# Moving the work between the matrix products of two mixer layers into and beside other stages

## The reference, cut to what matters

```python
h = rmsnorm(x, norm1_g[l])
u = einsum('btd,de->bte', h, w_in[l])                  # 3592 columns
(mq, mk, mv, mo, mi, mf, aq, ak, av, hq, hf, hi, hg) = split(u)
y_m = mlstm_mixer(mq, mk, mv, mo, mi, mf, ...)          # 4 heads of 64
y_a = diff_attention(aq, ak, av, ...)                   # 4 heads of 2 maps of 64, values of 128
y_h = hgrn2_mixer(hq, hf, hi, hg, ...)                  # 4 heads of 64
x = x + einsum('bte,ed->btd', concat([y_m, y_a, y_h]), w_out[l])
h2 = rmsnorm(x, norm2_g[l])
x = x + einsum('btf,fd->btd', square(relu(h2 @ w_up[l])), w_down[l])
```

## Time and profile before

| | us |
|---|---|
| median of 3 runs | 4036.71 (4032.25 to 4044.81) |
| the profiled execution | 4039.2 |
| its span, first to last instruction | 4037.4 |
| PE busy | 3690.6 (91%) |
| DVE, ACT, POOL busy | 1445.7, 1004.3, 1495.3 |
| DMA | 360.53 MB, mean 89 GB/s |

### The profile page before, as it was taken

How to read it: one execution, slowest core, us unless ns; L and a number is a source line. 1 busy time by engine, 2 the same in 40 slices (tenths; PEclk the granted TensorE clock), 3 DMA queues, 4 the chain that set the end, 5 groups by cost and what they waited for, 6 DMA issues and landing times.

```text
span 4037.4 us, 41511 instructions
## 1 busy us (share of the span) xinstructions
PE 3690.6 (91%) x16098; PEld 2831.0 (70%) x16098; DVE 1445.7 (36%) x2693; ACT 1004.3 (25%) x1287; POOL 1495.3 (37%) x557
## 2 busy tenths in 40 slices
PE   8999998899999998999998986679999986679999
PEld 7878785488878886457887873346888873346887
DVE  5453477242434223332101167442110167442110
ACT  2222324322222222022222233222222233222221
POOL 3445540144545453004455421013555420014553
PEclk9999998999999999899999997669999997669999
DMA  6434220143534331202222220002222220002221
GB/s 243 182 147 151 94 77 18 53 156 130 198 109 178 131 125 62 84 21 84 90 100 92 84 73 1 0 6 78 94 94 101 86 73 1 0 11 73 95 104 73
DMA packets 53861, 360.53 MB, mean 89 GB/s; under 512 B 5968, under 2 KB 6352, under 8 KB 16592
## 3 DMA queue, kind: packets, MB, share of 16 engines
q1 hardware_dynamic: 53712, 358.53, 24.5%
HBM read 356.41 MB, written 2.10 MB: 89 GB/s over the span
## 4 chain that ended last, share of the span: by engine, by line
PE 84%; DVE 10%; ACT 3%; issue 2%; POOL 1%; DMA 1%; SPq 0%; DVEq 0%; POOLq 0%; ACTq 0%
PE LP L424 74%; PE XB L424 8%; DVE rstd L1444 1%; DVE ada_in L1444 1%; PE XB L614 1%; DVE S L1636 1%; DMA big<-w_ada 1%; PE LP L730 1%; ACT L892 0%; ACT sq L892 0%; DVE big L1883 0%; ACT E L892 0%; DVE tmp L1767 0%; DVE st L1765 0%; POOL S L1324 0%
## 5 line engine op out<-in xcount | busy, mean ns | idle before, releaser
L1248 POOL TENSOR_TENSOR w_lo<-ring,w_hi 128x2048 fp32r<-128x2048 f32 (+1 forms) x263 | 1124.6, 4276 | 697.3 <-ACT w_hi L892 696.2
L424 PE MATMUL LP<-u_hi,w_hi 128*128 128x512 f32 x2480 | 989.0, 399 | 21.2 <-ACT u_hi L892 17.0
L424 PE MATMUL LP<-u_hi,w_lo 128*128 128x512 f32 x2480 | 979.1, 395 | 0.0
L424 PE MATMUL LP<-u_lo,w_hi 128*128 128x512 f32 x2480 | 936.8, 390 | 0.0
L424 PE MATMUL LP<-big_r,w_hi 128*128 128x512 f32 x2432 | 749.7, 389 | 1.2 <-POOL w_lo L1248 1.2
L892 ACT ACTIVATE w_hi<-ring 128x2048 fp32r<-128x2048 f32 (+1 forms) x263 | 468.9, 1783 | 965.2 <-PE LP L424 877.6
L424 PEld LDWEIGHTS LP<-u_hi,w_hi 128*128 128x128 f32 x2480 | 474.8, 191 | 124.6 <-issue 26.4
L424 PEld LDWEIGHTS LP<-u_hi,w_lo 128*128 128x128 f32 x2480 | 474.4, 191 | 101.6
L424 PEld LDWEIGHTS LP<-u_lo,w_hi 128*128 128x128 f32 x2480 | 466.5, 188 | 95.5 <-issue 0.5
L424 PEld LDWEIGHTS LP<-big_r,w_hi 128*128 128x128 f32 x2432 | 456.0, 188 | 95.6 <-issue 1.3
L424 PE MATMUL LP<-big_r,w_lo 128*128 128x512 f32 x1216 | 473.2, 389 | 0.0
(11 more groups left out here) (237 smaller groups left out, 3479.6 us busy)
## 6 DMA issues: line engine op xcount, KB each, us to landing
ada_in<-w_ada SPq DMA_DIRECT2D x66, 1024.0 KB, 4.9
ring<-w_in SPq DMA_DIRECT2D x22, 1024.0 KB, 4.8
ring<-w_gu00a SPq DMA_DIRECT2D x11, 1024.0 KB, 7.1
ring<-w_gu00b SPq DMA_DIRECT2D x11, 1024.0 KB, 6.7
ring<-w_gu01a SPq DMA_DIRECT2D x11, 1024.0 KB, 6.7
ring<-w_gu01b SPq DMA_DIRECT2D x11, 1024.0 KB, 6.6
ring<-w_gu10a SPq DMA_DIRECT2D x11, 1024.0 KB, 6.7
ring<-w_gu10b SPq DMA_DIRECT2D x11, 1024.0 KB, 6.9
```

The costliest lines, as they stand in the source:

```text
L424: return pe.matmul(o, lhsT=lhsT, rhs=rhs, start=start, stop=stop)
L1248: gp.tensor_tensor(w_lo[:, slab % RING, 0:width], ring[:, slab % RING, 0:width], w_hi[:, q % 2, 0:width].bitcast(F32), ALU.subtract).then_ ...
```

## The change

- `in` is loaded and computed in another order (`IN_ORDER`): gates first, then aq and ak, hf, hq, mq, mk, hg, mo. Its loop is unrolled.
- In the middle of a slab (`amid`) and behind it (`after`) PE gets small products. In `in`: slabs 2 to 5 rotate two chunks of q or k each and sum the squares of two; slabs 5 to 7 spread the eight inverse norms. The norms are kept as 8 rows (`half_sums` is a [128, 8] weight), so that Sqrt and RECIPROCAL work on [8, 512]; the norm's gain is applied where the slab is taken out, and the inverse norm is multiplied in behind the rotation.
- The gates, the recurrence's sigmoids, logarithm and sums, the convolutions and silus follow their slabs.
- The recurrence works on both pairs of heads at once (tiles of [128, 2, 512], `Z`). Levels 0 to 7 stand behind slabs 7 to 10 of `in` and 0 to 3 of `inv`, with the two halves j taken in turn (16 matmuls a level). Levels 8 and 9 and the product with v are placed in attention, behind the scores of units 0, 2, 4 and 6, in `LP[1]`.
- The mlstm loop uses `LP[0]`, `LP[1]`, XB[0] to XB[2]; `den` is a matmul with 4 columns of weights. The norms of attention's output and of the recurrence stand in this loop as 8 rows (`mix_norms`: 6 matmuls of sums behind unit 5, 6 of spreading behind units 8 to 13).
- `wo` no longer waits for everything: the 12 matmuls of slab 0 and then of slab 1 that don't use mlstm's chunks run while its division and norm are worked out as 4 rows.

What it takes away: `square_sums`, `root_one`, `rms_each`, `norm_qk`, the ten steps for each cp, the waits and norms between the stages.

The diff, cut to its core:

```diff
+                def qk_sums(pair):
+                    pe.wait_ge(s("qk_squared"), 4 * l + pair + 1)
+                    if pair == 2:
+                        pe.wait_ge(s("qk_root"), 2 * l + 1)
+                    for i in range(2):
+                        c = 2 * (pair % 2) + i
+                        last = mm(XB[0][0:8, :], half_sums(c, 8), big[:, 22 + c, :], start=c == 0, stop=c == 3)
+                    if pair % 2:
+                        last.then_inc(s("qk_summed"), 1)
+                def qk_spread(i):
+                    if i % 4 == 0:
+                        pe.wait_ge(s("qk_recip"), 2 * l + i // 4 + 1)
+                    if i == 0:
+                        pe.wait_ge(s("a_taken"), l + 1)
+                    else:
+                        pe.wait_ge(s("qk_scaled"), 8 * l + (i if i < 5 else i - 1))
+                    mm(XB[0 if i in (5, 7) else 3][:, :], halves_of(i % 4), qk_rows(i // 4)).then_inc(s("qk_spread"), 1)
...
+                def level(step):
+                    if step:
+                        pl.got("z_ready")
+                    else:
+                        pe.wait_ge(s("qk_scaled"), 8 * (l + 1))
+                        pl.got("h_k")
+                        pl.got("h_q")
+                    for cp in range(2):
+                        if step:
+                            pe.wait_ge(s("level_taken"), 2 * (8 * l + step - 1) + cp + 1)
+                        z = Z[:, 2 * (step % 2) + cp, :]
+                        for b in range(NB):
+                            for j in range(2):
+                                r, bank = half(j), XB[2 * cp + j]
+                                if step == 0:
+                                    last = mm(bank[:, blk(b)], big[r, SP + cp, blk(b)], big[r, HQ + cp, blk(b)])
+                                else:
+                                    last = mm(bank[:, blk(b)], z[r, blk(b)], z[r, blk(b)])
+                        last.then_inc(s("level_mm"), 1)
+                def amid_slab(k):
+                    if k == 5:
+                        qk_spread(1)
+                    if 2 <= k < 6:
+                        slab_taken(k - 1)
+                        rotate((AQ + 2 * k - 4, AQ + 2 * k - 3), cc("rot16"))
+                        qk_sums(k - 2)
...
+                        qk_spread(6)
+                        qk_spread(7)
+                def behind_slab(k):
+                    if k == 4:
+                        qk_spread(0)
+                    if k == 5:
+                        qk_spread(2)
+                    if k == 6:
+                        qk_spread(4)
+                        qk_spread(5)
+                    if k >= 7:
+                        level(k - 7)
+                linear(f"in{l}", "fm", src, after=behind_slab, fresh=fresh, amid=amid_slab)
+                linear(f"inv{l}", "tm", src, after=lambda k: level(k + 4))
...
+                def far_levels(n):
+                    if n == 0:
+                        pl.got("z_ready")
+                        for cp in range(2):
+                            for b in range(2):
+                                for j in range(2):
+                                    z = Z[half(j), cp, :]
+                                    o = 256 * cp + P * b
+                                    last = mm(LP[1][:, j, o:o + P], z[:, blk(2 * b)], z[:, blk(2 * b + 1)])
+                        last.then_inc(s("far_mm"), 1)
+                    if n in (2, 4):
+                        cp = n // 2 - 1
+                        if cp == 0:
+                            pl.got("z_ready")
+                        pe.wait_ge(s("far_taken"), 3 * l + cp + 1)
...
+                        pe.wait_ge(s("far_taken"), 3 * l + 3)
+                        for cp in range(2):
...
+                                if b < NB - 1:
+                                    o = (0, 384, 640)[b]
+                                    for j in range(2):
+                                        mm(LP[1][half(j), cp, (b + 1) * P:T], v[j],
+                                           OD[cp][:, j, o:o + (NB - 1 - b) * P], start=False, stop=False)
+                        last.then_inc(s("h_out"), 1)
+                pe.wait_ge(s("level_taken"), 16 * (l + 1))
+                attention(DIFF_H, diff_score, lambda hh, b: av[:, b, blk(hh)], P, maps=2, beside=far_levels)
+                pe.wait_ge(s("o_taken"), pl.head)
+                pl.got("h_mix")
...
+                def mix_norms(n):
+                    if n == 5:
+                        pl.got("mix_squared", 3)
+                        for c in range(DIFF_H):
+                            mm(XB[3][0:8, :], full_sums(c, 8), Z[:, c, :], start=c == 0, stop=False)
+                        for cp in range(2):
+                            last = mm(XB[3][0:8, :], half_sums(2 + cp, 8), tabs[:, 2 + cp, :], start=False, stop=cp == 1)
+                        last.then_inc(s("mix_summed"), 1)
+                    if 8 <= n < 14:
+                        i = n - 8
+                        if i == 0:
+                            pl.got("mix_recip")
+                        else:
+                            pe.wait_ge(s("mix_scaled"), 6 * l + i)
+                        weights = cc("ident")[0:8, i:i + 1].to_broadcast([8, P]) if i < DIFF_H else halves_of(i - 2)
+                        mm(XB[3][:, :], weights, mix_rows).then_inc(s("mix_spread"), 1)
...
+                def out_products(k, chunks):
+                    slab, group = pl.slab + k, pl.group + k
+                    slot, p = slab % RING, group % 2
+                    if chunks[0] == 2:
+                        pe.wait_ge(s(f"lin_taken{p}"), group // 2)
+                        pe.wait_ge(s(f"w_in{slot}"), 16 * (slab // RING + 1))
+                    for c in chunks:
+                        for f in range(2):
+                            last = mm(LP[p][:, f, :], ring[:, slot, c * 256 + f * P:c * 256 + f * P + P], u[:, c, :],
+                                      start=c == 2, stop=c == 1)
+                    if chunks[-1] == 1:
+                        last.then_inc(s("lin_done"), 1)
...
+                pl.got("h_gated", 2)
+                out_products(0, range(2, DC))
+                pl.got("num_squared")
+                    last = mm(XB[3][0:4, :], half_sums(cp, 4), Z[:, cp, :], start=cp == 0, stop=cp == 1)
+                last.then_inc(s("num_summed"), 1)
+                out_products(1, range(2, DC))
+                pl.got("num_recip")
...
+                def squares_of(k, it):
+                    if 1 <= k < 5:
+                        act.wait_ge(s("lin_done"), pl.slab + k + 1)
+                        c = 22 + 2 * ((k - 1) % 2)
+                        f(big[:, c:c + 2, :], LP[(first + k) % 2][:, :, :], ACT.Square).then_inc(s("qk_squared"), 1)
...
+                def level_exp(step):
+                    pl.got("x_ready")
+                    z = Z[:, 2 * (step % 2):2 * (step % 2) + 2, :]
+                    f(z, z, ACT.Exp).then_inc(s("ex_ready"), 1)
...
+                    if k == 5:
+                        slab_taken(k)
+                        f(big[:, SP:SP + 2, :], big[:, HF:HF + 2, :], ACT.Sigmoid, scale=-1.0).then_inc(s("scalar_chain"), 1)
+                        pl.got("scalar_chain")
+                        in_place(HF, ACT.Sigmoid).then_inc(s("h_sig"), 1)
+                        pl.got("h_f")
+                        f(big[:, 22:24, :], big[:, HF:HF + 2, :], ACT.Ln).then_inc(s("h_lnf"), 1)
+                    if k == 6:
...
+                def level_inputs(step):
+                    pl.got("ex_ready")
+                    b, p = 1 << (step - 1), 2 * (step % 2)
+                    z, kk, q = (t.rearrange("p c (j i b) -> p (c j) i b", i=2, b=b) for t in
+                                (Z[:, p:p + 2, :], big[:, SP:SP + 2, :], big[:, HQ:HQ + 2, :]))
+                    gp.tensor_tensor(z[:, :, 0, :], z[:, :, 0, :], kk[:, :, 0, :], ALU.mult)
+                    gp.tensor_tensor(z[:, :, 1, :], z[:, :, 1, :], q[:, :, 1, :], ALU.mult)\
+                        .then_inc(s("z_ready"), 1)
...
+                def exponents(step):
+                    b, p = 1 << (step - 1), 2 * (step % 2)
+                    Bv, X = (t.rearrange("p c (j i b) -> p (c j) i b", i=2, b=b)
+                             for t in (big[:, HF:HF + 2, :], Z[:, p:p + 2, :]))
+                    ref = Bv[:, :, 0, b - 1:b].to_broadcast([P, T // b, b])
+                    tt(X[:, :, 0, :], ref, Bv[:, :, 0, :], ALU.subtract)
+                    tt(X[:, :, 1, :], Bv[:, :, 1, :], ref, ALU.subtract).then_inc(s("x_ready"), 1)
...
+                def take_level(step):
+                    for cp in range(2):
+                        k = 2 * (8 * l + step) + cp
+                        dve.wait_ge(s("level_mm"), k + 1)
+                        ad, bk = (t[:, 2 * cp:2 * cp + 2, :].rearrange("p j (b t) -> p (j b) t", b=NB) for t in (AD, XBS))
```

(61 more changed lines are left out.)

510 lines of the change are left out of this document (241 added, 269 removed).

## The result

The changed kernel takes 3773.55 us (median of 4 runs, 3769.08 to 3776.09) and the kernel before, beside it on the same chip, 4034.72. The ratio is 0.9347, with a 95% interval of 0.9328 to 0.9366. So the forecast of 3807 us named the sign and most of the size (230 of 261 us); the time lies inside the range of 3745 to 3870 and 33 us under the likeliest value. The profiled execution took 3773.3 us, its span is 3771.5.

The account below looks back on a forecast made before the run. Handshakes between four engines were taken to bound the layer's middle, with PE full elsewhere. Six stages sum to 421.5 us a layer against 536.5, saving 115, 230 in all: 3807 us forecast, range 3745 to 3870.

Parts of the forecast that it names:

- the small matmul: Levels in `in` and `inv`: 16 matmuls each, K = 64, 128 columns, at 0.22 us; 28 us for eight levels.
- the changeover: `in` and `inv`: going from fp32r to small fp32 products and back, 0.3 us at some 19 places, 6 us.
- the reserve of 3 for stalls: `in` and `inv`: 3 us kept for stalls in case DVE and POOL collide, raising 226 to 229 us.
- The lower bound that I named: Levels: 0.135 us a matmul, from interleaved value products of 64 array columns, would give 17 us instead of 28.
- a level costs 3.5: Levels in `in` and `inv`: 16 small matmuls take 3.5 us a level, 28 us for all eight.
- The 9 added: Attention: levels 8 and 9, the product with v and DVE copies add 4 to 14 us, taken as 9, to 57.
- The 13 of the sum: mlstm loop: 12 more matmuls of 512 columns cost near 13 us at the mixed clock, 44 + 13 = 57.
- 44 at 0.75, and 11.3 of full-clock work: mlstm loop: 44 us at clock 0.75 would be 34 at the high clock; 12 added matmuls cost 11.3 there.
- Denser PE: Rival: overlapping halves save 11 us in levels, high clock 11 in mlstm, attention 5; 27 a layer, 3755 us; chance 0.17.
- Low clock in the slabs: Rival: each of eight levels brings half a slab at low clock in `in`/`inv`, 27 us a layer, 3861; chance 0.15.
- DVE and POOL: Rival: these engines become the bound, collisions cost 3 us more per slab over nine slabs, 27 a layer, 3861; chance 0.10.
- Slower: Rival: each of nine slabs waits for the levels' whole chain, about 14.5 us, 130 a layer; 4067 us; chance 0.04.

Follow-up runs that it names:

- the filled kernel: Changed kernel plus PE multiplying constants into an unused bank wherever it waited in attention's second half and mlstm's opening; 3780.94 us, ratio 0.9359.
- with one product: Changed kernel with mlstm's numerator and denominator from one matmul of 128 weight columns; 3783.27 us against 3772.64, ratio 0.9353.

## Why the prediction was right, and where it was off

1. *What bounds.* The handshakes of the recurrence and of the norms, 34 to 58 us each in the earlier trace rows, could be put beside PE's products, and PE's own work then sets the time. The run with the levels behind the slabs (+22 us a layer in that stage) and the one with `wo` behind the norm (+10 a layer) show both covers by undoing them. With the far levels behind attention, the three bring back 93 to 113 of the 261 us, what their mlstm loops lose included. What the narrow norms, kept as 8 rows, and the joint work on both pairs of heads bring was not undone by a run of its own.
2. *`in` and `inv`.* Predicted 229 and 2.5, measured 211.8 and 213.0 to the first score. This is where the 33 us are: 19 a layer. The term that was mis-sized is the small matmul, 0.22 each. Measured 0.129, and from each level's start to the next instruction's the eight take 16.0 us and not 28: 12. The second is the changeover, 0.3 at 19 places, for which I had no row, and with it the reserve of 3 for stalls, 9 together. By the same count the slab products with all changeovers take 170.6 and 171.8 us in the two layers, so 2.1 and 3.3 in place of 9: 7.0 and 5.7 less. (19 times the measured 0.15 is 2.9. PE idles for 0.1 us.) With 0.8 at the way into attention that is 19.8 and 18.5, the whole difference. Rotations, sums and spreads take 22.6, as forecast. The lower bound that I named, 0.135 from the value products, was the right row. I passed it over for one that seemed to have the shape of the levels, and that one was misread: four matmuls of 128 columns by my count, but two of them had 256. Read rightly it gives 0.14 too, and 18 for the eight levels. So the number for the overlap stood in my own rows, and "a level costs 3.5" was a wrong step, though it left the time inside the range.
3. *The way into attention.* PE waits 1.70 us; forecast 2.5.
4. *Attention.* 67.2 with the opening at 4.8; forecast 66 and 5. The 9 added were 10.
5. *The mlstm loop.* Forecast 57 by a clock of 0.75; measured 59.9 at 0.75 and 54.9 at 0.83. The 13 of the sum are too few for that clock: 11.3 / 0.75 = 15.1, which gives 59, near layer 0. That the average of both layers, 57.4, meets the 57 is luck. The step "44 at 0.75, and 11.3 of full-clock work" gives 33 + 11.3 = 44.3 us of work; measured 44.6. That denominators save nothing by having 4 columns holds.
6. *`wo`.* 60.7 against 62. It begins in the same moment as the loop ends, and the only wait is the bubble of 1.31 us. The chain that it covers is 13.6 us, not 9, under the 21 of cover.

The two layers are 17.1 and 21.7 us under 421.5, together 39. The sum of the prediction gave 3809 and the profiled execution took 3773.3: 36. So outside the two layers it takes 3 us more than forecast.

*The rivals.* "Denser PE" was to bring 11 a layer by overlapping halves, 11 by a high clock in the loop and 5 in attention. The 11 of the levels came in full (12), by just this overlap; of the rest only the 2 of layer 1's loop. "Low clock in the slabs" didn't come: 0.99, although eight levels with K = 64 stand in them. "DVE and POOL" was near: 0.6 us free in a slab with a convolution. "Slower" was far: even in the open a level costs 5 us, not 14.5, with the pair of buffers and no cut in POOL's queue between them.

*What stays open.* Why the clock falls in the loop while PE is full, and why it fell in just the measure in which work was taken away: 34 to 35 us of work at 0.59 in both layers of two kernels, 44 us at 0.69 to 0.83. That the fall is tied to the matmuls of this loop and not to gaps alone is shown by the filled kernel; which property of them does it (their fp32 passes, their size, the changes between shapes) wasn't separated. The levels, with K = 64 too, keep 0.99 among the slabs.

## What to carry to other kernels

Before a row of the timeline becomes a price, ask for the same stretch by shape: one row joined matmuls of 128 and of 256 columns, and the price taken from it was too high by more than half. When PE is full, multiply its busy time by the granted clock before and after an edit: if work goes and the clock goes with it, the time stays. And an edit of the work ahead of a stretch with an unsteady clock can make that stretch longer, here by up to 9.5 us in untouched code, so judge an edit by its own stage as well as by the total.

## What the runs showed of the hardware that I had not expected

- PE busy for all of its time doesn't hold the clock at 1.00: with one product the loop has 59.10 of 60 us busy and 0.59.
- Matmuls in different halves of the array overlap in fp32 too: row halves 2.06 us for 16 of 128 columns with every record paired, 2.82 with 9 of 16 pairs left, column halves 0.79 against 1.52 us for two of 384 columns.
- The low clock of attention comes from gaps of 0.4 to 3.2 us between short matmuls: 0.71 with them, 0.97 when they are filled. The time of attention with its opening hardly falls with it: 72.0 and 71.1 us against 71.2 in both layers.
